# Running sums of the gate logs as split fp32r products in a two-block transformer kernel

## What is computed

```python
f = lb_d + (1.0 - lb_d) * jax.nn.sigmoid(heads(f_pre))
gates.append((1.0 - f, jnp.log(f)))
...
b = jnp.cumsum(log_f.reshape(B, H, N, HG_CHUNK, DK), axis=3)
b_last = b[:, :, :, -1:, :]
q_dec = q * jnp.exp(b)
k_inv = k * jnp.exp(-b)
...
scores = jnp.einsum('bhnck,bhnsk->bhncs', q_dec, k_inv)
...
kv_chunk = jnp.einsum('bhnsk,bhnsv->bhnkv', k * jnp.exp(b_last - b), v)
```

## Time and profile before

| | us |
|---|---|
| median of 3 runs (lowest, highest) | 2600.96 (2600.3, 2600.99) |
| the profiled execution's own time | 2600.4 |
| its span | 2598.6 |
| TensorE busy | 2576.3 (99%) |
| VectorE busy | 1838.8 (71%) |
| ScalarE busy | 1361.8 (52%) |
| GpSimd busy | 176.9 (7%) |

### The profile page before, as it was taken

The page is one execution under the profiler, slowest core; times in us unless marked ns, Lnnn a source line. Parts: engine busy times, 40 slices in busy tenths (PEclk is TensorE's granted clock), DMA queues, the critical chain, the costliest instruction groups (busy, mean ns, idle before and its releaser), DMA issues.

```text
span 2598.6 us, 35433 instructions
## 1 busy us (share of the span) xinstructions
PE 2576.3 (99%) x13200; PEld 2173.1 (84%) x13200; DVE 1838.8 (71%) x3327; ACT 1361.8 (52%) x2613; POOL 176.9 (7%) x233
## 2 busy tenths in 40 slices
PE   8999999999999999999999999999999999999999
PEld 7999889888888888888888898888788888888887
DVE  5677665777799999676867775677866665555555
ACT  5445575655545445455766566565544444444443
POOL 1011100021100000000011100000001111000000
PEclk9999999999999999999999999999999999999999
DMA  9796665688888888866777755544577777565564
GB/s 304 236 296 184 209 202 171 188 287 278 290 284 270 277 285 271 308 191 219 237 242 236 247 175 153 156 131 153 162 233 257 255 253 224 186 195 188 188 193 161
DMA packets 315707, 582.98 MB, mean 224 GB/s; under 512 B 30176, under 2 KB 38384, under 8 KB 315408
## 3 DMA queue, kind: packets, MB, share of 16 engines
q1 hardware_dynamic: 296768, 559.94, 66.0%
q0 software_dynamic: 18480, 20.47, 3.6%
q10 hardware_dynamic: 288, 0.31, 0.0%
HBM read 574.35 MB, written 2.10 MB: 222 GB/s over the span
## 4 chain that ended last, share of the span: by engine, by line
PE 96%; DVE 1%; ACT 1%; SPq 0%; DMA 0%; issue 0%; DVEq 0%; ACTq 0%
PE ps L1838 27%; PE ps L1840 26%; PE ps L1839 26%; PE ps L1827 3%; PE ps L1828 3%; PE ps L1829 3%; PE ps L1784 2%; PE ps L1920 1%; PE ps L1890 1%; PE ps L1909 1%; DMA raw<-in_w_in 0%; DVE wlo L2495 0%; PE ps L2035 0%; ACT whi L2157 0%; PE ps L2052 0%
## 5 line engine op out<-in xcount | busy, mean ns | idle before, releaser
L2495 DVE TENSOR_TENSOR wlo<-raw,whi 128x512 fp32r<-128x512 f32 x1712 | 1098.2, 686 | 536.5 <-ACT whi L2157 534.0
L2157 ACT ACTIVATE whi<-raw 128x512 fp32r<-128x512 f32 x1712 | 982.0, 624 | 817.1 <-PE ps L1840 527.1
L1838 PE MATMUL ps<-whi,th 128*128 128x512 f32 (+1 forms) x3124 | 1230.9, 394 | 2.2 <-ACT hA L2351 1.0
L1840 PE MATMUL ps<-whi,tl 128*128 128x512 f32 (+1 forms) x3124 | 1211.2, 388 | 0.0
L1839 PE MATMUL ps<-wlo,th 128*128 128x512 f32 (+1 forms) x3124 | 1210.3, 387 | 0.0
L1838 PEld LDWEIGHTS ps<-whi,th 128*128 128x128 f32 x3124 | 586.9, 188 | 122.2 <-issue 5.1
L1840 PEld LDWEIGHTS ps<-whi,tl 128*128 128x128 f32 x3124 | 586.5, 188 | 121.7
L1839 PEld LDWEIGHTS ps<-wlo,th 128*128 128x128 f32 x3124 | 587.4, 188 | 115.7 <-issue 1.0
L2513 DVE SCALAR_TENSOR_TENSOR acc<-raw,silc,acc 128x512 f32<-128x512 f32 x480 | 343.9, 746 | 10.5 <-DMA raw<-in_w_mod 6.0
L1827 PE MATMUL ps<-th,whi 128*128 128x256 f32 x640 | 186.0, 291 | 11.0 <-DVE wlo L2495 8.1
L1828 PE MATMUL ps<-th,wlo 128*128 128x256 f32 x640 | 181.6, 284 | 0.0
(11 more groups left out here) (320 smaller groups left out, 1296.7 us busy)
## 6 DMA issues: line engine op xcount, KB each, us to landing
raw<-in_w_in SPq DMA_DIRECT2D x231, 512.0 KB, 3.9
raw<-in_w_down SPq DMA_DIRECT2D x216, 512.0 KB, 4.6
raw<-in_w_mod SPq DMA_DIRECT2D x192, 512.0 KB, 4.5
raw<-in_w_gate_up SPq DMA_DIRECT2D x176, 512.0 KB, 3.5
raw<-in_w_up SPq DMA_DIRECT2D x128, 512.0 KB, 4.6
raw<-in_w_out SPq DMA_DIRECT2D x64, 512.0 KB, 3.8
raw<-in_xattn_wkv SPq DMA_DIRECT2D x16, 512.0 KB, 3.4
raw<-in_w_in SPq DMA_DIRECT2D x16, 268.0 KB, 4.1
```

The costliest lines, as they stand in the source:

```text
L1838: pe.matmul(p, xh, wh[:, c, c0:n], start=a and (form != "both" or tb == 0), stop=False, skip_group_check=True)
L1840: ins = pe.matmul(p, xl, wh[:, c, c0:n], start=False, stop=z, skip_group_check=True)
L2157: self.e.activation(t.his[g % NHI][:, n * c:n * c + n], t.raws[j % NRAW][:, n * c:n * c + n], ACT.Copy).then_inc(*s.hi.up((g, c)))
L2495: self.e.tensor_tensor(t.los[j % NRAW][:, at], t.raws[j % NRAW][:, at], t.his[g % NHI][:, at].bitcast(F), ALU.subtract).then_inc(*s.lo.up( ...
```

## The change

The latents' logs are split into halves as those of the context are, into new buffers: `gh` (over the cross attention's context keys and values, which are done with by then) and `gl` (in place, over `hA`). The split takes the `yield` that was empty for latents. `forget_b` multiplies both halves with `hgmR`; `head_turned` takes the halves as stationary tiles, with a rounded copy `chkR` of the two chunk masks moving, so that its sums are four fp32r products in place of two fp32 ones. `chkR` is made once, at the first latent gate. Both now wait for the low half (`fl`) in place of the logarithm (`f4`).

```diff
+        self.chkR, self.gh, self.gl = sb("chkR", r_y, [2, 128], R), sb("gh", z + 34816, [2, 512], R), sb("gl", r_s, [2, 512], R)
...
         self.gate_logs(key)
         yield
+        self.gate_split(key, latent)
+        yield
         if not latent:
-            self.gate_split(key)
             yield
             yield
-        yield
         for tb in [d] if latent else range(2):
...
+            if n == 0:
+                self.chunk_masks([(s.q7, k) for k in ('lk', 'lq0', 'lq1')])
...
-                    self.g_after = [(s.h0, last)]
+                    self.g_after = self.gh_after = [(s.h0, last)]
...
     def forget_b(self, key, tb, d, latent, bank):
         if latent:
-            self.wait_ge(*s.f4.at(key))
-            ins = pe.matmul(bank.tile[:, :], t.hgmR[:, d, :].bitcast(F), t.hA[:, tb, :], start=True, stop=True, skip_group_check=True)
+            self.wait_ge(*s.fl.at(key))
+            pe.matmul(bank.tile[:, :], t.hgmR[:, d, :], t.gh[:, tb, :], start=True, stop=False, skip_group_check=True)
+            ins = pe.matmul(bank.tile[:, :], t.hgmR[:, d, :], t.gl[:, tb, :], start=False, stop=True, skip_group_check=True)
...
-        self.wait_ge(*s.f4.at(u["key"]))
+        self.wait_ge(*s.fl.at(u["key"]))
         self.wait_ge(*s.f3.at(u["key"]))
+        self.wait_ge(*s.hgr.at(2))
         for tb in range(2):
-            pe.matmul(e[:, 128 * tb:128 * tb + 128], t.hA[:, tb, hs], t.hgm[:, u["d"], :], start=True, stop=True, skip_group_check=True)
+            for half, z in ((t.gh, 0), (t.gl, 1)):
+                pe.matmul(e[:, 128 * tb:128 * tb + 128], half[:, tb, hs], t.chkR[:, u["d"], :], start=z == 0 and tb == 0, stop=z == 1,
+                          skip_group_check=True)
...
+    def chunk_masks(self, used):
+        self.wait_all(used)
+        self.e.activation(t.chkR[:, :, :], t.hgm[:, 0:2, :], ACT.Copy).then_inc(*s.hgr.up(2))
...
-        self.wait_all(self.fh_after)
-        self.e.activation(t.fh[:, :, :], t.hA[:, :, :], ACT.Copy).then_inc(*s.fh.up(key))
+        self.wait_all(self.gh_after if latent else self.fh_after)
+        self.e.activation((t.gh if latent else t.fh)[:, :, :], t.hA[:, :, :], ACT.Copy).then_inc(*s.fh.up(key))
...
-        self.e.tensor_tensor(t.fl[:, :, :], t.hA[:, :, :], t.fh[:, :, :].bitcast(F), ALU.subtract).then_inc(*s.fl.up(key))
+        hi, lo = (t.gh, t.gl) if latent else (t.fh, t.fl)
+        self.e.tensor_tensor(lo[:, :, :], t.hA[:, :, :], hi[:, :, :].bitcast(F), ALU.subtract).then_inc(*s.fl.up(key))
```

More of the change, by code:

```diff
@@ L362 @@
     hidden_out = hidden_turn = silu_out = prod_out = mod_gain = final_scale = final_square = gate_row = skip
-    bound_diff = gate_sigmoids = gate_scale = gate_keys = gate_logs = forget_b = forget_c = ctx_state = scan_ones = head_turned = head_states = head_outputs = skip
+    bound_diff = gate_sigmoids = gate_scale = gate_keys = gate_logs = forget_b = forget_c = ctx_state = scan_ones = chunk_masks = head_turned = head_states = head_outputs = skip
     read_silu = head_square = head_scale = head_back = head_low = rope_tables = gate_split = masks_rounded = qk_out = qk_sums = qk_norm = qk_rot = qk_turn = sink_neg = skip
@@ L1569, in run @@
         self.scan_ones()
+        self.gh_after = scrL
         gate = lambda g, d: self.gemm(op1, w2, 0, 1024 + 1024 * d + 512 * g, 512, range(16), self.lat_gate(g, d, op2m))
@@ L2361, in gate_logs @@
         self.e.activation(t.hA[:, :, :], t.hA[:, :, :], ACT.Ln).then_inc(*s.f4.up(key))
+    def chunk_masks(self, used):
+        t, s = self.t, self.s
+        self.wait_all(used)
+        self.e.activation(t.chkR[:, :, :], t.hgm[:, 0:2, :], ACT.Copy).then_inc(*s.hgr.up(2))
     def masks_rounded(self, used):
@@ L2369, in masks_rounded, with gate_split @@
         self.e.activation(t.oneR[:, :], t.ones[:, :], ACT.Copy).then_inc(*s.hgr.up(1))
-    def gate_split(self, key):
+    def gate_split(self, key, latent):
         t, s = self.t, self.s
         self.wait_ge(*s.f4.at(key))
-        self.wait_all(self.fh_after)
-        self.e.activation(t.fh[:, :, :], t.hA[:, :, :], ACT.Copy).then_inc(*s.fh.up(key))
+        self.wait_all(self.gh_after if latent else self.fh_after)
+        self.e.activation((t.gh if latent else t.fh)[:, :, :], t.hA[:, :, :], ACT.Copy).then_inc(*s.fh.up(key))
     def forget_b(self, key, tb, d, latent, bank):
```

## The result

| | median us | lowest to highest | runs |
|---|---|---|---|
| before | 2600.97 | 2600.2 to 2603.01 | 20 |
| after | 2606.18 | 2604.53 to 2607.43 | 20 |

The ratio is 1.0019, with a 95% interval of 1.0013 to 1.0025, that is 3.4 to 6.5 us: slower by 5.2 us, about the size that a measurement of this kernel can tell from none. The forecast was 2605.2, in a range of 2602.4 to 2612.8. The profiled execution of after took 2606.55, its span is 2604.7.

What follows compares the result with a forecast made beforehand. TensorE, never waiting from 1600 to 1800 us, was taken as the bound. Terms -1.6 + 0.2 + 5.6 = +4.2 us on the profiled 2600.4, with the median 0.56 higher, gave 2605.2; range 2602.4 to 2612.8.

Steps and rivals of the forecast that it cites:

- Part 1: Column sums in forget_b: two fp32r products replace one fp32 product in each of four latent gates, -1.6 us.
- Part 2: Chunk sums in head_turned, 16 heads: four fp32r products cost about two fp32 ones, +0.2 us (-0.2 to +0.6).
- Part 3: Split into halves: TensorE waits for gl at forget_b in the latent gates, 2.7, 1.4, 0.1, 1.4, together +5.6 us.
- (A): Rival: fp32r products of 128 columns in head_turned are slow, handled like fp32; +11.0 in all, 2612.0 us; chance 0.30.
- (B): Rival: short fp32r products load weights faster, at the transposes' 0.07; +1.4 in all, 2602.4 us; chance 0.06.
- (C): Rival: TensorE does not wait at forget_b because the split is done earlier; -1.4 in all, 2599.6 us; chance 0.04.
- (D): Rival: the waits at forget_b are long enough for TensorE's clock to fall; more than the forecast, unpriced; chance 0.04.

Runs made afterwards that it cites:

- wait filled: Changed kernel with idle fp32 products ahead of the waiting column sum, three in the first latent gate, one in the others: 2605.78 us, ratio 1.0018.
- split at once: Changed kernel with the split in the logarithm's own step, ahead of the next chunk's weight halves; column sum stays: 2602.22 us, ratio 1.0006.
- no split: Changed kernel without the split: the logarithm writes gh itself, each fp32r pair multiplies gh twice, low half left out: 2599.22 us, ratio 0.9992.
- needed half first: Changed kernel with logarithm and split by halves of 128x512, the half forget_b reads first, in one step: 2599.37 us, again 2599.68.
- one more step: Changed kernel with one more step (a chunk of 12 products) between split and column sum of the latent gates: 2601.11 us, ratio 1.0000.
- chunk sums fp32: Changed kernel with head_turned put back to two fp32 products, of gh only, per head: 2606.57 us, ratio 1.0021.
- wait alone: Changed kernel keeping split and wait, but with fp32 products of gh only in forget_b and head_turned: 2608.37 us, ratio 1.0026.
- one less: Changed kernel with the column sum one step (2.7 us) earlier, right behind the split: 2632.31 us, ratio 1.0120.

## Why the prediction was right, and where it was not

- **Part 1, -1.6.** Right: 0.41 a gate, read in the kernel without a wait.
- **Part 2, +0.2.** Mis-sized: it measured -0.3, inside its outer bounds and a little outside the -0.2 to +0.6. One record each and 0.11 apart were right, the pace of a weight load in the earlier trace rows. The term had charged all four products with 0.107 or more, but the first takes only 0.06, about what its columns ask for (a quarter of 0.226): its weights were loaded during the long product ahead (1635.13 to 1635.35), as the load records show.

```profile
1635.13 0.19 PEld L2042 LDWEIGHTS ps<-chkR,gh 128*128 128x128 f32 x1
1635.36 0.19 PEld L2042 LDWEIGHTS ps<-chkR,gl 128*128 128x128 f32 x1
```

  The row of 15 columns has such a short first one too, 0.03, and the others 0.112 apart; the mean, 0.107, hid it. That "the load sets the pace in both" is not shown for before: a record of an fp32 product takes 0.43 for 512 columns, so 0.107 for 128 by its columns alone, and there the first of the four takes 0.11 like the others.
- **Part 3, +5.6.** The waits are 2.70, 1.41, about 0.05 and 1.42 where 2.7, 1.4, 0.1 and 1.4 stood. This was no luck: the context gates show the same series in the same order, and it took 4.45 us again. The restart of a waiting pair adds 0.08 three times. -1.6 - 0.3 + 5.6 + 0.2 = +3.9, beside +4.1 on the stretch. No wait for a weight half came behind it.
- **(A)** given 0.30, and **(B)**, 0.06: both fell. For (B) the Trainium skill's 81 ns a pair ("TensorE: Matmul & The Clock Gate", section "Back-to-back issue gap") is not what this kernel shows; its pitch within a group is 0.11.
- **(C):** it needed a split 2.7 us earlier. Splitting at once takes the first wait from 2.54 to 1.65, and splitting by halves as well to 0.26.
- **(D)** given 0.04 and no price: partly true, and the weakest step of the prediction. It argued that 2.2 us of idle time had left the clock at 1.00 and that 2.7 was hardly more. Five profiles have this wait (2.54 in the bracket) in the first gate, and four of them show the fall behind it; it costs 1.5 to 1.6 us. The ten waits of 1.26 in the second and fourth gates of the same five show none. Behind 1.65 us (one profile), behind 0.26 (two), and with the wait filled (one), none shows it; behind 5.3 to 6.5 us each of four does, in one profile.

The argument against (D) read one profile of a wait that all 13 have. Between 27 and 31 us TensorE waits for a `tl` in each (before, changed, and the eleven of the experiments), for 1.65 to 3.94 us, and the clock falls within 1.2 us behind it in six: after 1.76, 1.98, 2.03, 2.94, 3.44 and 3.94. It stays at 1.00 after 1.65, 1.73, 2.23 (the one of before), 2.31, 2.68, 3.25 and 3.30. Two of those in which it stayed show a fall behind the next wait, of 1.85, at 47 us. With the chunk sums in fp32 it fell after 1.76, with the wait filled it stayed after 3.30:

```profile
30.17 0.36 PE L1831 MATMUL ps<-th,whi 128*128 128x256 f32 x1 [1.76 <-DVE tl L2496]
...
30.00:34.00 4.00, 3.83 (x22) 3.86 (x23) 2.20 (x5) 4.00 (x7) 0.00 (x0) 0.67 1.03 375
```

```profile
30.57 0.36 PE L1831 MATMUL ps<-th,whi 128*128 128x256 f32 x1 [3.30 <-DVE tl L2500]
...
30.00:34.00 4.00, 3.11 (x24) 2.93 (x24) 2.44 (x6) 4.00 (x7) 0.00 (x0) 1.00 1.03 379
```

So in this range the length of a wait does not decide by itself, and a single profile without a fall excludes nothing, no more than the 1.65 us of the split at once.

That (D) is the missing microsecond of the median fits the two sums side by side. It is not shown: the interval of each experiment's median is 2.3 us either way, wider than the microsecond in question. "Stretch" is from one profile of each kernel, "median" is the difference of the medians to before.

| kernel | stretch | of it the fall | median |
|---|---|---|---|
| no split | -1.9 | 0 | -1.9 |
| needed half first (two runs) | -1.4, -1.4 | 0 | -1.7, -1.2 |
| one more step | +0.1 | 0 | 0.0 |
| split at once | +1.3 | 0 | +1.1 |
| wait filled | +4.6 | 0 | +4.7 |
| changed (three runs) | +4.1, +5.6, +5.7 | 0, 1.5, 1.6 | +5.2, +4.9, +5.7 |
| chunk sums fp32 | +5.8 | 1.6 | +5.4 |
| wait alone | +7.4 | 1.6 | +7.2 |

Without a fall stretch and median agree within 0.3. The changed kernel's three medians lie between its stretch without the fall and the one with it (the third at the upper end), the two other kernels with this wait a little under theirs with it. What decides in which executions the fall comes is left open; with the same wait to the hundredth the changed kernel had it in two and not in one.

## What to carry to other kernels

Where one engine never idles, count in order what stands between the last input and the product that needs it, on each engine's queue: 1.9 us of cheaper products were paid for with 5.6 us of waiting, and nearly all of it came back by splitting the needed half first, not by another step in the plan (one more step removed the wait and lost its gain elsewhere; one less ended 31 us above before). Even with the needed half first the median is not clear of before: the stretch says -1.4, the intervals of both runs reach past 1.0000. Look at a new wait of TensorE for what may come behind it as well as for its sum: 1.8 to 4 us in one piece lowered the granted clock for the work behind it in some profiles and not in others. Before you argue from a wait that did no harm, look for the same wait in other profiles of the kernel. When a profile's own time and the median differ by a microsecond, compare one stretch bounded by the same instructions in both kernels.

## What the runs showed of the hardware

- Fp32r products of 128 columns are one record each; behind a long product the first takes 0.06 us and the others are 0.11 apart, so two of them cost no more than one fp32 product (0.40 for four, 0.44 for two fp32 ones).
- After 2.7 us without work, TensorE's granted clock stood at 0.5, the 1.2 GHz level, for about 3.4 us in four of five profiles; fp32r products of 512 columns then ran 0.43 apart in place of 0.23. After 5.3 to 6.5 us of waiting it stood there at each of four gates, with 4.2 to 5.1 us of work in it.
- A wait near 30 us, 1.65 to 3.94 us long, was followed by such a fall in 6 of 13 profiles, one of them after 1.76 us; in one it stayed away after 3.30 us.
- After a wait the first fp32r product of a pair takes 0.30 to the next, not 0.23.
